# Stick-breaking attention: the sums over later keys from two rounded parts, and scores two heads ahead

## The chip, the cores and the metric

The kernel runs on one core of one Trainium2 chip. The metric is the device time of the whole program in microseconds (us), the median of several runs. A core has TensorE (PE in the rows; its weight loads are PEld), VectorE (DVE), ScalarE (ACT), GpSimd (POOL) and SyncE (SP). They run side by side, each through its own list of instructions in order, and wait for each other on semaphores.

## What is computed

The program is two transformer blocks of two layers each on 512 tokens of width 1024. The change touches one part alone, the stick-breaking attention in the first layer of the second block: 8 heads of dimension 64, 512 queries, 512 keys, in blocks of 128.

```
def stick_breaking_attention(q, k, v):
...
        z = jnp.einsum('bqhd,bkhd->bhqk', q[:, t0:t1], k[:, :t1]) * (HEAD_DIM ** -0.5)
        causal = jnp.arange(t1)[None, :] < (t0 + jnp.arange(SB_BLOCK))[:, None]
        log_fail = jnp.where(causal, -jax.nn.softplus(z), 0.0)
        log_after = lax.cumsum(log_fail, axis=3, reverse=True) - log_fail
        a = jnp.where(causal, jnp.exp(jax.nn.log_sigmoid(z) + log_after), 0.0)
        outs.append(jnp.einsum('bhqk,bkhd->bqhd', a, v[:, :t1]))
```

For each head: scores z, softplus(z), a sum of softplus over all later keys (and the key itself), a = exp(z - that sum), and a times the values. The same layer has eight heads of sliding-window attention beside it, whose output is transposed for the output projection while the stick-breaking heads run.

## The kernel before

Every engine has a program of its own (`pe_sb`, `act_sb`, `dve_sb`), written out by hand in rounds i. Nothing reorders it: what stands first in an engine's list runs first, and an instruction that waits holds up all that is behind it. `K.at(key)` names the semaphore count at which a result is there. PE writes to 8 PSUM banks, handed out in a ring; a bank is reused once DVE or ACT has freed it.

A head has, with keys on the partitions and queries along the row, 1280 columns: 512 + 384 + 256 + 128 for the key blocks 0 to 3, which fill three banks (`SB_BANKS`). Its steps:

- `sb_scores(h)`, PE: per bank one matmul that adds the causal mask and the matmuls of keys by queries, into `sb_z`.
- `dve_zs(h)`, DVE: three copies of the scores from PSUM into z. z has four buffers, s two (`sb_mem`).
- ACT: Abs, Exp, a table load, Ln, on all 1280 columns: s = log(1 + exp(-|z|)), key `sb_ln`.
- DVE: s = max(z, 0) + s, which is softplus, key `sb_sp`.
- `sb_after(h)`, PE: the sum over later keys, ten fp32 matmuls over 2560 columns in all, with a triangle of ones within a key block and a matrix of ones for the blocks after it. An fp32 matmul has two records in the trace.
- DVE: z = z - that sum, three pieces, key `sb_loga`. ACT: a table load and Exp, key `sb_a`.
- `sb_product(h)`, PE: four fp32 matmuls of values by a, 64 rows of bank `abT` 4 + h // 2; two heads fill one.

Beside it `pe_ab_turn(k)`, k 0 to 3, transposes a quarter of the sliding-window output on PE into bank `abT` k, and each of the eight `abT` is taken out by ACT (`act_ab_hi`, a copy rounded to fp32r, the rounded form that TensorE takes in one pass) and then by DVE (`dve_ab_lo`, the rest of it). `sb_blocks(i)` says which k ACT and DVE take out at the head of round i.

In round i of before, PE does after(i-1), product(i-2), turn(i-1) and scores(i+1). ACT does `act_ab_hi` of the blocks, then Abs to Ln of head i, then Exp of head i-1. Block k < 4 is taken out in round k+2. Heads, blocks and rounds count from 0; "after(i)" below is `sb_after` of head i, "hi(k)" is `act_ab_hi` of block k, "ln(i)" is ACT's row Abs, Exp, table load, Ln of head i.

Of the kernel before, what the change touches and what calls it, by code (L numbers as in the profile page):

```python
# [8 lines left out]
F32 = mybir.dt.float32  # L9
# [6 lines left out]
MUL, ADD, SUB, MAX, MIN = ALU.mult, ALU.add, ALU.subtract, ALU.max, ALU.min  # L16
# [2580 lines left out]
def ab_out(K):  # L2597
    return K.mem(W1, 2048).rearrange("p (t n) -> p t n", n=512)
# [42 lines left out]
def act_ab_proj(a, K):  # L2641
    qk, q5, k5, va, qb5, kb5, vb = ab_mem(K)
    cs, gr, snk, posi, posf, ang, kk, sn, co = ab_small(K)

    def feat(tag, dst, f, by):
        a.wait_ge(*K.at(tag, f, 0))
        a.cp(dst[:, f, :], K.ps(tag, f, 0)[:, :], scale=by).then_inc(*a.sig((tag, "out")))
        a.free(tag, f, 0)

    a.wait_ge(*K.at("ab"))  # L2650
    us = cs[:, 256:384]
    for dst, src in zip(sw_mask(K), (K.ident, cs[:, 0:256])):
        a.cp(dst, src).then_inc(*a.sig("sw_mask"))
    for o, by in ((0, 1.0), (128, 0.0), (256, 0.0), (384, 1.0), (512, 0.0), (640, 0.0), (768, 0.0)):
        a.cp(K.rx[:, 8576 + o:8704 + o], us, scale=by).then_inc(*a.sig("sb_mask"))
    for i, dst in enumerate((sn, co)):
        a.wait_ge(*K.at("ab_ang", i))
        a.act(dst, dst, ACT.Sin).then_inc(*a.sig("ab_sin"))
    a.tile()
    act_tok_out(a, K, "ab_q", range(4), lambda t: qk[:, t, 0:512])  # L2660
    a.tile()
    a.tile()
    for t in range(4):
        ps = K.ps("ab_k", t)
        a.wait_ge(*K.at("ab_k", t))
        a.cp(qk[:, t, 512:640], ps[:, 0:128]).then_inc(*a.sig(("ab_qk", t)))
        a.cp(va[:, t, :], ps[:, 128:256]).then_inc(*a.sig())
        a.free("ab_k", t)
    for f in range(4):
        if f % 2 == 0:  # L2670
            a.tile()
        a.root(K.tmpc[:, 60:70], ("ab", f))
        feat("ab_qb", qb5, f, 0.125)
    for f in range(4):
        if f % 2 == 0:
            a.tile()
        feat("ab_kb", kb5, f, 1.0)
    for k in range(0, 6, 2):
        a.wait_ge(*K.at("ab_T", k))
        a.cp(q5[:, k, :] if k < 4 else k5[:, k - 4, :], K.ps("ab_T", k)[:, :]).then_inc(*a.sig("ab_T_a"))  # L2680
        a.free("ab_T", k)
    for kh in range(2):
        a.tile()
        for t in range(4):
            if kh:
                a.wait_ge(*K.at("ab_vb", t))
                a.cp(vb[:, t, :], K.ps("ab_vb", t)[:, :]).then_inc(*a.sig("ab_vb_out"))
                a.free("ab_vb", t)
            for i in (kh * 8 + t * 2, kh * 8 + t * 2 + 1):
                act_sw(a, K, i)  # L2690
    for i in (16, 17):
        act_sw(a, K, i)
# [90 lines left out]
def sw_mask(K):  # L2783

    return K.rx[:, 8192:8320], K.rx[:, 8320:8576]
# [104 lines left out]

SB_COL = {0: 0, 1: 512, 3: 896, 2: 1024}
SB_BANKS = [(1, 3), (2,), (0,)]
SB_ROUNDS = range(11)


def sb_size(kb):
    return 512 - 128 * kb


def sb_part(j):  # L2900

    o = SB_COL[SB_BANKS[j][0]]
    return slice(o, o + sum(sb_size(kb) for kb in SB_BANKS[j]))


def sb_mask(K, j):

    o, n = ((8576, 512), (8960, 256), (8960, 512))[j]
    return K.rx[:, o:o + n]


def sb_mem(K, h):

    return K.mem(SWW + (6960, 416, 4256, 5536)[h % 4], 1280), K.mem(SWW + (1696, 2976)[h % 2], 1280)


def sb_bank(K, tag, h, j):
    c = sb_part(j)
    return K.ps(tag, h, j)[:, 0:c.stop - c.start]


def sb_scores(p, K, h):
    qk, q5, k5, va, qb5, kb5, vb = ab_mem(K)
    pr = slice(h % 2 * 64, h % 2 * 64 + 64)
    if h == 0:
        p.wait_ge(*K.at("ab_kb", "out"))
        p.wait_ge(*K.at("sb_mask"))
    for j, kbs in enumerate(SB_BANKS):
        b, c = p.bank("sb_z", h, j), sb_part(j)
        p.mm(b[:, 0:c.stop - c.start], sw_mask(K)[0], sb_mask(K, j), True, False)  # L2930
        for kb in kbs:
            o, n = SB_COL[kb] - SB_COL[kbs[0]], sb_size(kb)
            ins = p.mm(b[:, o:o + n], kb5[pr, h // 2, kb * 128:kb * 128 + 128], qb5[pr, h // 2, kb * 128:512], False,
                       kb == kbs[-1])
        ins.then_inc(*p.sig(("sb_z", h, j)))
        p.close("sb_z", h, j)


def sb_after(p, K, h):
    s = sb_mem(K, h)[1]  # L2940
    p.wait_ge(*K.at("sb_sp", h))
    for j, kbs in enumerate(SB_BANKS):
        b = p.bank("sb_after", h, j)
        for kb in kbs:
            o, n = SB_COL[kb] - SB_COL[kbs[0]], sb_size(kb)
            ins = p.mm(b[:, o:o + n], K.tri[1], s[:, SB_COL[kb]:SB_COL[kb] + n], True, kb == 3)
            for k2 in range(kb + 1, 4):
                ins = p.mm(b[:, o + (k2 - kb) * 128:o + n], K.ones, s[:, SB_COL[k2]:SB_COL[k2] + sb_size(k2)], False, k2 == 3)
        ins.then_inc(*p.sig(("sb_after", h, j)))
        p.close("sb_after", h, j)  # L2950


def sb_product(p, K, h):

    vb, a = ab_mem(K)[6], sb_mem(K, h)[0]
    k, pr = 4 + h // 2, slice(h % 2 * 64, h % 2 * 64 + 64)
    if h == 0:
        p.wait_ge(*K.at("ab_vb_out"))
    if h % 2 == 0:
        if h:  # L2960
            p.close("abT", k - 1)
        p.bank("abT", k)
    b = K.ps("abT", k)
    p.wait_ge(*K.at("sb_a", h))
    for kb in range(4):
        n = sb_size(kb)
        ins = p.mm(b[pr, kb * 128:512], vb[:, kb, h * 64:h * 64 + 64], a[:, SB_COL[kb]:SB_COL[kb] + n], kb == 0, kb == 3)
    ins.then_inc(*p.sig(("abT", k) if h % 2 else ("sb_o", h)))
    if h == 7:
        p.close("abT", k)  # L2970


def pe_sb(p, K):
    sb_scores(p, K, 1)
    for i in SB_ROUNDS:
        if 0 <= i - 1 < 8:
            sb_after(p, K, i - 1)
        if 0 <= i - 2 < 8:
            sb_product(p, K, i - 2)
        if 1 <= i < 5:  # L2980
            pe_ab_turn(p, K, i - 1)
        if 2 <= i + 1 < 8:
            sb_scores(p, K, i + 1)


def sb_blocks(i):

    return [k for k in range(8) if i == (k + 2 if k < 4 else 2 * k - 4)]


def act_sb(a, K):
    for i in SB_ROUNDS:
        for k in sb_blocks(i):
            act_ab_hi(a, K, k)
        if i < 8:
            z, s = sb_mem(K, i)
            if i >= 2:
                a.wait_ge(*K.at("sb_after", i - 2, 2))
            a.wait_ge(*K.at("sb_zs", i))
            a.act(s, z, ACT.Abs).then_inc(*a.sig())  # L3000
            a.act(s, s, ACT.Exp, scale=-1.0).then_inc(*a.sig())
            a.act(s, s, ACT.Ln, bias=1.0).then_inc(*a.sig(("sb_ln", i)))
        if 0 <= i - 1 < 8:
            z = sb_mem(K, i - 1)[0]
            a.wait_ge(*K.at("sb_loga", i - 1))
            a.act(z, z, ACT.Exp).then_inc(*a.sig(("sb_a", i - 1)))


def dve_zs(v, K, h):
    z = sb_mem(K, h)[0]  # L3010
    if h >= 4:
        v.wait_ge(*K.at(*(("abT", 4 + (h - 4) // 2) if h % 2 else ("sb_o", h - 4))))
    for j in range(3):
        v.wait_ge(*K.at("sb_z", h, j))
        v.cp(z[:, sb_part(j)], sb_bank(K, "sb_z", h, j)).then_inc(*v.sig(("sb_zs", h)))
        v.free("sb_z", h, j)


def dve_sb(v, K):
    dve_zs(v, K, 0)  # L3020
    for i in SB_ROUNDS:
        for k in sb_blocks(i):
            dve_ab_lo(v, K, k)
        if 0 <= i - 1 < 8:
            z = sb_mem(K, i - 1)[0]
            for j in range(3):
                c = sb_part(j)
                v.wait_ge(*K.at("sb_after", i - 1, j))
                v.tt(z[:, c], z[:, c], sb_bank(K, "sb_after", i - 1, j), SUB).then_inc(*v.sig(("sb_loga", i - 1)))
                v.free("sb_after", i - 1, j)  # L3030
        if i < 8:
            z, s = sb_mem(K, i)
            v.wait_ge(*K.at("sb_ln", i))
            v.stt(s, z, 0.0, s, MAX, ADD).then_inc(*v.sig(("sb_sp", i)))
        if i + 1 < 8:
            dve_zs(v, K, i + 1)

# [1 line left out]
def pe_ab_turn(p, K, k):  # L3041
    p.wait_ge(*K.at("sw_out", 15))
    b = p.bank("abT", k)
    for t in range(4):
        ins = p.tr(b[:, t * 128:(t + 1) * 128], ab_out(K)[:, t, k * 128:(k + 1) * 128])
    ins.then_inc(*p.sig(("abT", k)))
    p.close("abT", k)
# [1396 lines left out]
```

## Time and profile before

| | us |
|---|---|
| median of 3 runs | 4309.4 |
| lowest, highest | 4307.35, 4322.24 |
| the profiled execution | 4309.93 |
| its span, from the first to the last instruction | 4307.7 |
| its stick-breaking part, from scores(1) on PE to the first matmul of the output projection | 2658.5 to 2750.0 |

Times in the rows are microseconds from the span's start unless marked ns. What lies between the span and the time of the execution is 2.2 us. A group of instructions shows the form (partitions x columns) of its first one, so a row of 20 matmuls named 128x384 mixes widths. PEclk is the clock granted to TensorE: 1.00 is 2.4 GHz, 0.50 is 1.2 GHz.

### The profile page before, as it was taken

To read this page: it belongs to the slowest core of one execution; us is meant where nothing else is said; L and a number is where in the kernel's file an instruction comes from. 1 tells how busy PE (TensorE), PEld (TensorE's weight loads), DVE (VectorE), ACT (ScalarE), POOL (GpSimd) and SP (SyncE) were. 2 spreads that over 40 slices of the span, in tenths; PEclk is the share of its full clock that TensorE was granted. 3 is DMA by queue.
4 is the path that set the end of the run, shared out by engine and by line. 5 is a ranking of instruction groups with operands and counts; after the bars stand their busy time and mean duration, and the time that the engine had idled before them with its cause. 6 is when DMAs were issued, how large, how long until landed. Compare 5 with 4: busy or idle time off the path is not lost.

```text
span 4307.7 us, 67439 instructions
## 1 busy us (share of the span) xinstructions
PE 3920.8 (91%) x28266; PEld 3229.7 (75%) x28266; DVE 2097.2 (49%) x3022; ACT 1606.8 (37%) x2639; POOL 561.3 (13%) x628
## 2 busy tenths in 40 slices
PE   6988897878999998988899889989999998899999
PEld 4866785766888776756688676678888887678887
DVE  3545454656212353277423664554655428545564
ACT  3333333333111233164323345644334336544333
POOL 0035303642000001002100000000220003000220
PEclk8978898888999999999899999999999999999999
DMA  4234433131212121102232230131223230322332
GB/s 154 81 129 143 147 96 116 32 109 45 73 59 67 51 85 59 58 2 93 70 94 93 79 87 10 52 118 50 94 93 103 88 115 6 119 69 70 98 98 88
DMA packets 248534, 355.08 MB, mean 82 GB/s; under 512 B 9299, under 2 KB 158502, under 8 KB 247846
## 3 DMA queue, kind: packets, MB, share of 16 engines
q1 hardware_dynamic: 233840, 300.49, 21.7%
q0 software_dynamic: 13840, 50.11, 3.7%
q8 instruction: 222, 3.64, 0.4%
q14 instruction: 82, 0.67, 0.1%
q10 hardware_dynamic: 550, 0.17, 0.0%
HBM read 336.50 MB, written 14.24 MB: 81 GB/s over the span
## 4 chain that ended last, share of the span: by engine, by line
PE 76%; DVE 12%; ACT 7%; POOL 2%; issue 2%; DMA 1%; ACTq 0%; DVEq 0%; SPq 0%; POOLq 0%
PE psum L233 20%; PE psum L234 20%; PE psum L235 20%; PE psum L230 13%; ACT arena L341 3%; DVE arena L264 3%; PE psum L239 3%; DVE rw L264 2%; DVE arena L274 2%; POOL arena L379 1%; ACT arena L345 1%; DVE rx L335 1%; ACT rw L345 1%; DVE arena L278 1%; DVE arena L270 1%
## 5 line engine op out<-in xcount | busy, mean ns | idle before, releaser
L233 PE MATMUL psum<-rx,rw 128*128 128x512 f32 (+2 forms) x2864 | 1047.8, 366 | 61.2 <-DVE rx L335 30.1
L234 PE MATMUL psum<-rx,rw 128*128 128x512 f32 (+2 forms) x2864 | 1029.7, 360 | 0.0
L235 PE MATMUL psum<-rx,rw 128*128 128x512 f32 (+2 forms) x2864 | 1028.2, 359 | 0.0
L230 PE MATMUL psum<-arena 32*32 32x32 f32 (+10 forms) x12982 | 810.3, 258 | 158.0 <-ACT arena L345 63.9
L264 DVE TENSOR_TENSOR rw<-arena,rw 128x2048 fp32r<-128x2048 f32 (+2 forms) x239 | 537.6, 2249 | 846.5 <-ACT rw L345 841.2
L230 PEld LDWEIGHTS psum<-arena 32*32 32x32 f32 (+5 forms) x12982 | 614.8, 142 | 334.1 <-issue 113.9
L345 ACT ACTIVATE rw<-arena 128x2048 fp32r<-128x2048 f32 (+2 forms) x239 | 448.1, 1875 | 769.2 <-PE psum L235 744.4
L233 PE MATMUL psum<-rw,rx 128*128 128x512 f32 (+1 forms) x1720 | 683.0, 397 | 53.0 <-DVE rx L335 35.8
L234 PE MATMUL psum<-rw,rx 128*128 128x512 f32 (+1 forms) x1720 | 676.3, 393 | 0.0
L235 PE MATMUL psum<-rw,rx 128*128 128x512 f32 (+1 forms) x1720 | 675.7, 393 | 0.0
L233 PEld LDWEIGHTS psum<-rx,rw 128*128 128x128 f32 (+1 forms) x2864 | 550.3, 192 | 159.7 <-DVE rx L335 42.6
L234 PEld LDWEIGHTS psum<-rx,rw 128*128 128x128 f32 (+1 forms) x2864 | 551.4, 193 | 80.8 <-issue 4.1
L235 PEld LDWEIGHTS psum<-rx,rw 128*128 128x128 f32 (+1 forms) x2864 | 550.2, 192 | 79.1
L345 ACT ACTIVATE arena<-psum 128x512 f32<-128x512 f32 (+6 forms) x675 | 313.9, 465 | 773.1 <-PE psum L235 415.1
L379 POOL TENSOR_TENSOR arena<-arena 128x512 f32<-128x512 f32 (+5 forms) x300 | 419.6, 1399 | 980.4 <-DVE arena L274 396.5
L233 PEld LDWEIGHTS psum<-rw,rx 128*128 128x128 f32 x1720 | 329.6, 192 | 128.6 <-DVE rx L335 40.8
L341 ACT ACTIVATE arena<-arena 128x512 f32<-128x512 f32 (+11 forms) x476 | 249.5, 524 | 468.6 <-DVE arena L274 219.2
L235 PEld LDWEIGHTS psum<-rw,rx 128*128 128x128 f32 x1720 | 328.9, 191 | 68.6
L234 PEld LDWEIGHTS psum<-rw,rx 128*128 128x128 f32 x1720 | 329.6, 192 | 66.2
L274 DVE SCALAR_TENSOR_TENSOR arena<-arena 128x512 f32<-128x512 f32 (+8 forms) x481 | 353.9, 736 | 44.4 <-ACT arena L341 27.8
L264 DVE TENSOR_TENSOR arena<-arena,psum 128x512 f32<-128x512 f32 (+3 forms) x308 | 151.8, 493 | 312.7 <-PE psum L235 205.1
L239 PE MATMUL psum<-arena 128*128 128x128 f32 (+2 forms) x1284 | 200.6, 296 | 102.7 <-DVE arena L264 32.9
(71 smaller groups left out, 2092.0 us busy)
## 6 DMA issues: line engine op xcount, KB each, us to landing
arena<-in_ffn_w_up SPq DMA_DIRECT2D x66, 1024.0 KB, 5.2
arena<-in_ada_w SPq DMA_DIRECT2D x48, 1024.0 KB, 5.2
arena<-in_ffn_w_down SPq DMA_DIRECT2D x40, 1024.0 KB, 5.0
arena<-in_ffn_w_gate SPq DMA_DIRECT2D x22, 1024.0 KB, 5.3
arena<-in_dn_w_in SPq DMA_DIRECT2D x32, 512.0 KB, 5.3
arena<-in_xa_w_kv SPq DMA_DIRECT2D x16, 1024.0 KB, 5.0
arena<-in_hgrn_w_in SPq DMA_DIRECT2D x16, 1024.0 KB, 5.4
arena<-in_da_w_in SPq DMA_DIRECT2D x12, 1024.0 KB, 5.1
```

Of the source, the lines that this page charges most:

```text
L230: return self.e.matmul(out, l, r, start=start, stop=stop)
L233: self.e.matmul(out, l[0], r[0], start=start, stop=False)
L234: self.e.matmul(out, l[0], r[1], start=False, stop=False)
L235: return self.e.matmul(out, l[1], r[0], start=False, stop=stop)
L239: return self.e.transpose(out, a, self.K.ident[0:k, 0:k])
L264: return self.e.tensor_tensor(out, a, b, op)
L270: return self.e.tensor_scalar(out, a, s1, s2, op0, op1)
L274: return self.e.scalar_tensor_tensor(out=out, in0=a, scalar=s, in1=b, op0=op0, op1=op1)
L278: return self.e.tensor_reduce(out, a, AX.X, op)
L341: return self.e.activation(out, a, f, **kw)
L345: return self.e.activation(out, a, ACT.Copy, **kw)
L379: return self.e.tensor_tensor(out, a, b, op)
```

## The change

Three things are done at once.

- `sb_after` no longer multiplies softplus in fp32. DVE rounds s to fp32r (hi, a cast), subtracts it from s and rounds the rest (lo), and PE does every matmul of the sum twice, with hi and with lo, as fp32r by fp32r copies of the triangle and of the ones, which ACT makes once, long before. Ten fp32 matmuls become twenty fp32r ones. There is one pair hi, lo, so the cast of head i waits until after(i-1) has read it.
- Scores run two heads ahead: PE does scores(i+2) at the head of round i and DVE `dve_zs(i+2)`. after(i) moves from round i+1 to round i, product(i-1) and turn(i) follow it, and ten rounds are left of eleven.
- `sb_blocks` moves up with it: block k < 4 is taken out in round k+1 (before k+2), block k > 3 in round 2k-5 (before 2k-4), still at the head of the round on ACT, ahead of ln(i).

```diff
+    for dst, src in zip(sb_split(K)[1:], (K.tri[1], K.ones)):
+        a.cp(dst, src).then_inc(*a.sig("sb_mask"))
...
+def sb_split(K):
+
+    at = [(9728, 1280), (11008, 1280), (9472, 128), (9600, 128)]
+    hi, lo, here, whole = [K.rx[:, o:o + n] for o, n in at]
+    return (hi, lo), here, whole
...
 def sb_after(p, K, h):
-    p.wait_ge(*K.at("sb_sp", h))
+    p.wait_ge(*K.at("sb_lo", h))
...
-            ins = p.mm(b[:, o:o + n], K.tri[1], s[:, SB_COL[kb]:SB_COL[kb] + n], True, kb == 3)
+            for i, s in enumerate(parts):
+                ins = p.mm(b[:, o:o + n], here, s[:, SB_COL[kb]:SB_COL[kb] + n], i == 0, i == 1 and kb == 3)
...
 def pe_sb(p, K):
     sb_scores(p, K, 1)
     for i in SB_ROUNDS:
+        if i + 2 < 8:
+            sb_scores(p, K, i + 2)
+        if i < 8:
+            sb_after(p, K, i)
         if 0 <= i - 1 < 8:
-            sb_after(p, K, i - 1)
-        if 0 <= i - 2 < 8:
-            sb_product(p, K, i - 2)
-        if 1 <= i < 5:
-            pe_ab_turn(p, K, i - 1)
-        if 2 <= i + 1 < 8:
-            sb_scores(p, K, i + 1)
+            sb_product(p, K, i - 1)
+        if 0 <= i < 4:
+            pe_ab_turn(p, K, i)
...
-    return [k for k in range(8) if i == (k + 2 if k < 4 else 2 * k - 4)]
+    return [k for k in range(8) if i == (k + 1 if k < 4 else 2 * k - 5)]
...
             if i >= 2:
-                a.wait_ge(*K.at("sb_after", i - 2, 2))
+                a.wait_ge(*K.at("sb_lo", i - 2))
...
 def dve_sb(v, K):
+    hi, lo = sb_split(K)[0]
     dve_zs(v, K, 0)
+    dve_zs(v, K, 1)
     for i in SB_ROUNDS:
         for k in sb_blocks(i):
             dve_ab_lo(v, K, k)
...
-            v.stt(s, z, 0.0, s, MAX, ADD).then_inc(*v.sig(("sb_sp", i)))
-        if i + 1 < 8:
-            dve_zs(v, K, i + 1)
+            v.stt(s, z, 0.0, s, MAX, ADD).then_inc(*v.sig())
+            if i:
+                v.wait_ge(*K.at("sb_after", i - 1, 2))
+            v.cp(hi, s).then_inc(*v.sig())
+            v.tt(lo, s, hi.bitcast(F32), SUB).then_inc(*v.sig(("sb_lo", i)))
+        if i + 2 < 8:
+            dve_zs(v, K, i + 2)
+        if i < 8:
+            for j in range(3):
+                c = sb_part(j)
+                v.wait_ge(*K.at("sb_after", i, j))
+                v.tt(z[:, c], z[:, c], sb_bank(K, "sb_after", i, j), SUB).then_inc(*v.sig(("sb_loga", i)))
```

ACT's list at the start of the part, with the semaphores that each waits for. Before: Abs, Exp, table, Ln of head 0, then Abs, table, Exp, table, Ln of head 1, the table and Exp that give a of head 0, and then the first block, hi(0):

```order
L341 ACTIVATE arena<-arena 128x1280 [waits s_act]
L341 ACTIVATE arena<-arena 128x1280 [waits s_act,s_dve]
L341 ACT_TABLE_LOAD
L341 ACTIVATE arena<-arena 128x1280 [waits s_act]
L341 ACT_TABLE_LOAD
L341 ACTIVATE arena<-arena 128x1280 [waits s_act]
L341 ACT_TABLE_LOAD [waits s_act]
L341 ACTIVATE arena<-arena 128x1280 [waits s_dve]
L345 ACTIVATE rx<-psum 128x512 [waits s_act,s_pe]
L341 ACTIVATE arena<-arena 128x1280 [waits s_act,s_dve]
```

Now the same place, from Ln of head 0 on:

```order
L341 ACTIVATE arena<-arena 128x1280 [waits s_act]
L345 ACTIVATE rx<-psum 128x512 [waits s_act,s_pe]
L341 ACTIVATE arena<-arena 128x1280 [waits s_act,s_dve]
L341 ACT_TABLE_LOAD
L341 ACTIVATE arena<-arena 128x1280 [waits s_act]
L341 ACT_TABLE_LOAD
L341 ACTIVATE arena<-arena 128x1280 [waits s_act]
L341 ACT_TABLE_LOAD [waits s_act]
L341 ACTIVATE arena<-arena 128x1280 [waits s_dve]
L345 ACTIVATE rx<-psum 128x512 [waits s_act,s_pe]
L341 ACTIVATE arena<-arena 128x1280 [waits s_act] x2
```

hi(0), the L345 row that waits for PE, moved from behind the Exp of head 0 to ahead of the Abs of head 1, and hi(1) from behind the Exp of head 1 to ahead of the Abs of head 2.

PE's list in the round of after(1). Before, after the fp32 sums, came the product of head 0 (64x512 to 64x128), the transposes of block 1 (L239) and the scores of head 3:

```order
L230 MATMUL psum<-arena 128x384 [waits s_dve]
L230 MATMUL psum<-arena 128x256
L230 MATMUL psum<-arena 128x128 x2
L230 MATMUL psum<-arena 128x256
L230 MATMUL psum<-arena 128x128
L230 MATMUL psum<-arena 128x512
L230 MATMUL psum<-arena 128x384
L230 MATMUL psum<-arena 128x256
L230 MATMUL psum<-arena 128x128
L230 MATMUL psum<-arena 64x512 [waits s_act]
```

Now the sums read rx, in pairs, and the product and the transposes follow them as before:

```order
L230 MATMUL psum<-rx 128x384 [waits s_dve]
L230 MATMUL psum<-rx 128x384
L230 MATMUL psum<-rx 128x256 x2
L230 MATMUL psum<-rx 128x128 x4
L230 MATMUL psum<-rx 128x256 x2
L230 MATMUL psum<-rx 128x128 x2
L230 MATMUL psum<-rx 128x512 x2
L230 MATMUL psum<-rx 128x384 x2
L230 MATMUL psum<-rx 128x256 x2
L230 MATMUL psum<-rx 128x128 x2
L230 MATMUL psum<-arena 64x512 [waits s_act]
```

On PE the order of the steps within a round stays; the numbers of the heads against ACT's and DVE's rounds shift by one.

## Rows read from the trace of the kernel before

**Rows 1.** The page: the span, and TensorE's busy time with its share
```profile
span 4307.7 us, 67439 instructions
...
PE 3920.8 (91%) x28266; PEld 3229.7 (75%) x28266; DVE 2097.2 (49%) x3022; ACT 1606.8 (37%) x2639; POOL 561.3 (13%) x628
```

**Rows 2.** Stretches: length, busy us (count) per engine, PEclk, DMA share, GB/s
```profile
2662.40:2667.70 5.30, 0.07 (x2) 0.03 (x1) 1.49 (x1) 3.66 (x3) 0.00 (x0) 0.77 0.00 0
2667.70:2672.10 4.40, 4.40 (x13) 3.44 (x14) 2.49 (x4) 2.32 (x2) 0.00 (x0) 0.50 0.00 0
2672.10:2750.00 77.90, 77.18 (x296) 44.66 (x295) 39.83 (x55) 57.96 (x50) 0.00 (x0) 1.00 0.00 1
2750.00:2800.00 50.00, 50.00 (x230) 41.64 (x230) 26.22 (x40) 24.92 (x45) 1.81 (x3) 1.00 0.35 111
```

**Rows 3.** The chain that ended last, in this part: start, us, what
```profile
2708.23 25.22 PE psum L230 x89
```

**Rows 4.** Timeline, PE: start, us, what, xcount, [idle before <-releaser]; first block, rounds' scores
```profile
2667.67 6.74 PE L230 MATMUL psum<-arena 128*128 128x384 f32 x20 [5.23 <-DVE arena L274]
...
2674.60 0.47 PE L230 MATMUL psum<-rx 128*128 128x512 f32 x1
...
2685.72 0.48 PE L230 MATMUL psum<-rx 128*128 128x512 f32 x1
```

**Rows 5.** Timeline, PE, short stretches: sums, product, transposes; the part's end
```profile
2678.48 4.60 PE L230 MATMUL psum<-arena 128*128 128x384 f32 x20
...
2683.01 2.37 PE L230 MATMUL psum<-arena 128*64 128x512 f32 x8
...
2685.31 0.66 PE L239 MATMUL psum<-arena 128*128 128x128 f32 x4
...
2740.99 9.05 PE L230 MATMUL psum<-arena 128*128 128x384 f32 x36 [0.72 <-DVE arena L274]
2749.97 0.50 PE L233 MATMUL psum<-rw,rx 128*128 128x512 f32 x1
```

**Rows 6.** Timeline, ACT: Abs and Exp of a head, a table load, and hi
```profile
2679.87 2.57 ACT L341 ACTIVATE arena<-arena 128x1280 f32<-128x1280 f32 x2 [0.35 <-DVE arena L290]
2682.46 1.28 ACT L341 ACT_TABLE_LOAD   x1
...
2687.76 0.60 ACT L345 ACTIVATE rx<-psum 128x512 fp32r<-128x512 f32 x1
2690.44 2.57 ACT L341 ACTIVATE arena<-arena 128x1280 f32<-128x1280 f32 x2 [2.09 <-DVE arena L290]
```

**Rows 7.** Timeline, DVE: softplus of heads 0 and 2
```profile
2666.12 1.49 DVE L274 SCALAR_TENSOR_TENSOR arena<-arena 128x1280 f32<-128x1280 f32 x1 [5.22 <-ACT arena L341]
...
2685.06 1.49 DVE L274 SCALAR_TENSOR_TENSOR arena<-arena 128x1280 f32<-128x1280 f32 x1 [1.25 <-ACT arena L341]
```

**Rows 8.** Timeline, PE: fp32r matmuls of 512, 256 and 128 columns, each with the next
```profile
2590.06 0.39 PE L233 MATMUL psum<-rw,rx 128*128 128x512 f32 x1
2590.29 0.40 PE L234 MATMUL psum<-rw,rx 128*128 128x512 f32 x1
...
2507.73 0.28 PE L233 MATMUL psum<-rw,rx 128*128 128x256 f32 x1
2507.85 0.28 PE L234 MATMUL psum<-rw,rx 128*128 128x256 f32 x1
...
2577.21 0.33 PE L230 MATMUL psum<-rx 128*128 128x128 f32 x1
...
2577.47 0.49 PE L230 MATMUL psum<-arena 64*128 64x128 f32 x2
```

**Rows 9.** Groups by form, DVE, 2600 to 4300: xcount | busy us, mean ns | idle
```profile
L264 DVE TENSOR_TENSOR rw<-arena,rw 128x2048 fp32r<-128x2048 f32 x120 | 275.1, 2293 | 273.6 <-ACT rw L345 270.3
...
L290 DVE COPY arena<-psum 128x512 f32<-128x512 f32 x60 | 41.5, 691 | 80.1 <-PE psum L235 59.9 <-PE psum L230 15.0 <-PE psum L239 2.8
...
L269 DVE TENSOR_SCALAR arena<-arena 128x1024 f32<-128x1024 f32 x24 | 18.1, 754 | 0.8
...
L264 DVE TENSOR_TENSOR rw<-arena,rw 128x1024 fp32r<-128x1024 f32 x4 | 4.9, 1225 | 25.2 <-ACT rw L345 25.2
...
L290 DVE COPY arena<-psum 128x256 f32<-128x256 f32 x8 | 3.4, 425 | 1.5 <-PE psum L230 1.3
```

**Rows 10.** Timeline, ACT: the nine mask copies at the start of the layer
```profile
2496.09 3.16 ACT L345 ACTIVATE rx<-arena 128x128 fp32r<-128x128 f32 x9
```

More of the change, by code:

```diff
@@ L2892 @@
 SB_BANKS = [(1, 3), (2,), (0,)]
-SB_ROUNDS = range(11)
+SB_ROUNDS = range(10)
 def sb_size(kb):
@@ L2939, in sb_after @@
 def sb_after(p, K, h):
-    s = sb_mem(K, h)[1]
-    p.wait_ge(*K.at("sb_sp", h))
+    parts, here, whole = sb_split(K)
+    p.wait_ge(*K.at("sb_lo", h))
     for j, kbs in enumerate(SB_BANKS):
@@ L2945, in sb_after @@
             o, n = SB_COL[kb] - SB_COL[kbs[0]], sb_size(kb)
-            ins = p.mm(b[:, o:o + n], K.tri[1], s[:, SB_COL[kb]:SB_COL[kb] + n], True, kb == 3)
+            for i, s in enumerate(parts):
+                ins = p.mm(b[:, o:o + n], here, s[:, SB_COL[kb]:SB_COL[kb] + n], i == 0, i == 1 and kb == 3)
             for k2 in range(kb + 1, 4):
-                ins = p.mm(b[:, o + (k2 - kb) * 128:o + n], K.ones, s[:, SB_COL[k2]:SB_COL[k2] + sb_size(k2)], False, k2 == 3)
+                for i, s in enumerate(parts):
+                    ins = p.mm(b[:, o + (k2 - kb) * 128:o + n], whole, s[:, SB_COL[k2]:SB_COL[k2] + sb_size(k2)], False,
+                               i == 1 and k2 == 3)
         ins.then_inc(*p.sig(("sb_after", h, j)))
@@ L3023, in dve_sb @@
             dve_ab_lo(v, K, k)
[L3024 to L3030, printed above, removed]
         if i < 8:
@@ L3033, in dve_sb @@
             v.wait_ge(*K.at("sb_ln", i))
-            v.stt(s, z, 0.0, s, MAX, ADD).then_inc(*v.sig(("sb_sp", i)))
-        if i + 1 < 8:
-            dve_zs(v, K, i + 1)
+            v.stt(s, z, 0.0, s, MAX, ADD).then_inc(*v.sig())
[10 more added lines that the diff above has]
+                v.tt(z[:, c], z[:, c], sb_bank(K, "sb_after", i, j), SUB).then_inc(*v.sig(("sb_loga", i)))
+                v.free("sb_after", i, j)
 def pe_ab_turn(p, K, k):
```

## The prediction

> **What bounds the kernel now.** The page says that PE is busy 91% of the span [rows 1], but the change lies in one part, so the part decides. Read the stretches first [rows 2]. From 2672.1 to 2750.0 PE is busy 77.2 of 77.9 us at full clock, while ACT is busy 58.0 and DVE 39.8; in the 50 us behind it PE is busy throughout. The chain of work that ended last agrees: it lies on PE for 25.2 us in one piece [rows 3]. The timeline of PE gives the beat: scores start at 2674.60 and again at 2685.72, one head per 11.1 us [rows 4]. The one large hole is at the start: PE idles 5.23 us for the softplus of head 0, and then the clock is 0.50 for 4.4 us [rows 2, 4]. Where is slack? ACT waits 2.1 us before the Abs of a head [rows 6], DVE 1.25 us before softplus [rows 7]. So shorter PE work pays until another engine, or a loop of waits through several engines, takes 11.1 us or more. That loop has to be looked for, since the change moves steps between rounds.
>
> **The sums on PE.** The old block starts at 2678.48 and the product behind it at 2683.01: 4.53 us [rows 5]. The new one has 20 fp32r matmuls: 2 of 512 columns, 4 of 384, 6 of 256, 8 of 128. From start to start a 512 takes 0.23, a 256 takes 0.12 [rows 8], so 384 lies at 0.175. Of 128 columns only one stands alone: 0.26 to an fp32 matmul behind it [rows 8], which bounds it from above; the four transposes of 128 columns with a weight load each start 0.11 apart ((0.66 - 0.33) / 3, where 0.33 is the length of one [rows 5, 8]). I take 0.11, between 0.07 (the columns alone, half of a 256) and 0.26. Sum: 0.46 + 0.70 + 0.72 + 0.88 = 2.8 us, and 0.2 to the fp32 product: 3.0 us, 1.5 less than before. By PE alone a round would be 11.1 - 1.5 = 9.6 us.
>
> **The new work on DVE.** Softplus takes 1.49 [rows 7]. The subtraction that gives lo has two inputs of 1280 columns; that kind takes 1.225 for 1024 and 2.293 for 2048 [rows 9], so 1.49. The cast of 1280 columns has one input: TENSOR_SCALAR of 1024 takes 0.754 [rows 9], in proportion 0.94 and less for the fixed part, so 0.88; the ceiling is the two-input pace, 1.49. I take 0.88, since it is the single-input row that is like it.
> The Trainium skill says the same ("VectorE: DVE Perf Modes", the perf-mode tier table: an fp32 copy within SBUF runs at two elements per cycle, one with two tensors at one); no run here shows it for an fp32r output. At one per cycle each loop below would be 0.6 us longer.
> Each step adds some 0.04 to 0.1 of waiting. DVE's round: lo of a block 0.79, softplus 1.53, cast 0.92, subtraction 1.55, three copies of scores 0.79 + 0.52 + 0.79, and three subtractions of the same size, 2.1 [rows 7, 9]: 9.0 us. That fits under 9.6.
>
> **The moved steps, and the wait they add.** ACT's hi(k), k < 4, now stands at the head of round k+1, ahead of ln(k+1). It waits for turn(k), which on PE stands behind after(k) and product(k-1). What is queued behind the waiting hi(k) on ACT is ln(k+1), then the Exp of head k; DVE waits for ln(k+1) with softplus, cast and lo of head k+1, and PE for those with after(k+1), with product(k) and turn(k+1) behind it. That closes a loop within one round. Before, hi(k) stood ahead of ln(k+2), and after(k+2) came two rounds later, so that the same steps had 22 us. Once round, at full clock:
>
> - after(k) and the gap: 3.0
> - product(k-1), start to turn(k): 2685.31 - 2683.01 = 2.3 [rows 5]
> - turn(k) 0.66 [rows 5], to ACT 0.1: 0.75
> - hi(k) 0.60 and 0.1 [rows 6]: 0.7
> - Abs to Ln: from 2679.87 to softplus at 2685.06 [rows 6, 7]: 5.2
> - softplus 1.53, cast 0.92, lo 1.55: 4.0
>
> Sum 15.95, say 15.9 us, against 11.1 before and 9.6 for PE alone. PE then idles 6.3 us in each such round, behind scores(k+3).
>
> Which rounds? 0 to 1: no product yet, 15.9 - 2.3 = 13.6. 1 to 2: 15.9. 2 to 3: two blocks (2 and 4) are taken out, 16.5. 3 to 4: 15.9. 4 to 5: hi(5) waits for product(3), which ends round 4 on PE, without a turn: 15.3. 5 to 6: no block; DVE's own row sets it (0.1 to 0.2 to each bank, the last subtraction 0.69, softplus to lo 4.0, after a block of 2.8): some 8.3. 6 to 7: hi(6) waits for product(5): 15.3. Sum 100.8. Tail from after(7): 2.9, the last bank's subtraction 0.8, Exp 1.3, product 2.2: 7.2, where before it was 2749.97 - 2740.99 = 9.0 [rows 5].
>
> Start: softplus of head 0 is ready to run at 2666.12 as before [rows 7]; the second dve_zs and scores(2) (3.9 us) lie in the idle 5.2 us. With cast and lo after(0) starts at 2670.1, 2.4 later than before (2667.67 [rows 4]). So at full clock the part ends at 2670.1 + 100.8 + 7.2 = 2778.1, against 2749.97: 28.1 us later.
>
> **The clock.** After 5.2 us of idling the first block before ran at 0.50 for 4.4 us [rows 2] and took 2674.24 - 2667.67 = 6.6 us to the transposes (6.74 with the overlap [rows 4], where a warm one has 4.60 [rows 5]): 2.1 us lost. Now PE idles 6.3 us or more ahead of after(i) for i = 1 to 5 and 7, and 4 us ahead of after(0), and all that follows, after, product and turn, is in the loop. Seven times 0 to 2.1; I take 1.9, near the one row there is: 13.3. The full-clock sum left the 2.1 of the first block out, so it counts here.
>
> **Small things.** Two more mask copies of 0.34 on ACT (3.16 / 9 [rows 10]), 150 us earlier, where ACT waits now and then: 0 to 0.7, taken as 0.3. No DMA, no POOL or SP work is moved; the loads for the next step wait for the last abT and shift with it. The product of this part is followed by the same full PE row as before, so nothing later gives the time back.
>
> **Sum.** 28.1 + 13.3 + 0.3 = 41.7. The profiled execution took 4309.93, 0.5 over the median; so 4351.6 in such an execution, 4351 for the median.
>
> **Rivals.**
> 1. The loop does not bind, PE does. For it: PE is the busiest engine of the part [rows 2], and every step is there and shorter. It would hold if hi(k) were ready when ACT comes to it; the loop decides from the point at which its sum is over 9.6 us, and it would have to lose 6.3. Against: the order of ACT's list, in which hi(0) stands ahead of the Abs of head 1. Time: start +2.4, seven rounds of 9.3 on average (9.6 with a turn, 9.0 on DVE without) 65, tail 7.2, first block's clock 2.1: the part ends at 2744.5, so 5 us earlier, 4304. This is the case on the other side: not slower.
> [...]
> 2. The loop binds, but PE's clock stays full, since PE works 9.6 of 15.9 us. Against: the one idle of this length went to 0.50 [rows 2]. 4338.
> 3. The loop binds and the narrow fp32r matmuls are no faster than the fp32 ones (0.26 each for 128 columns, 0.32 for 256): 1.5 us more in eight blocks, 4363.
>
> **How the numbers follow.** Forecast 0.75, rival 1 0.10, rival 2 0.08, rival 3 0.05, something else 0.02. Range: the cast at the two-input pace adds 8 x 0.6 = 5, narrow matmuls at 0.07 take 8 x 0.3 = 2.5 off, the clock 13 off or 2 on. From 4335, just under rival 2, to 4363, rival 3. Rival 1 is left out. A measurement of this kernel tells 0.5% (21.5 us) from no change; all loop cases are beyond it, rival 1 is within: slower 0.89, same 0.09, faster 0.02.
>
> **What would show it.** In the profile after: PE idle of some 6 us ahead of each after(i), released by DVE; ACT idle ahead of the L345 copies into rx, released by PE (L239, or L230 for the product); a beat of 16 to 18 us in the first five rounds; PEclk under 0.85 over the part; the sums 2.8 us where the clock is full; the cast 0.9. Wrong if the beat is under 11, if ACT does not wait ahead of hi(k), or if the sums take over 4 us at full clock.

## The result, and the profile after

| | before | after |
|---|---|---|
| median, us (5 runs each) | 4307.35 | 4349.04 |
| lowest, highest | 4294.20, 4322.24 | 4342.35, 4352.89 |
| the profiled execution | 4309.93 | 4349.75 |
| its part: scores(1) to the output projection | 2658.5 to 2750.0, 91.5 long | 2656.2 to 2793.05, 136.8 long |

The changed kernel takes 1.0094 times as long (a ratio of the runs' means; 95% interval 1.0072 to 1.0115), 41.7 us more by the medians and 39.8 more between the profiled executions. The part itself grew by 45.3 us. It began 2.3 us earlier, and what lies behind it took some 3 us less; both lie outside the change, and no cause was looked for. That work wanders by several microseconds from run to run: over all the profiled runs here scores(1) starts between 2647.9 and 2658.5. So below each version is judged by two things, its time and the length of its part in the trace; the second is the sharper.

The page after, against [rows 1]: PE is busy 6.6 us more, at 90% where it was 91%. At this height nothing is to be seen.

```profile
span 4347.5 us, 67450 instructions
...
PE 3927.4 (90%) x28266; PEld 3245.1 (75%) x28266; DVE 2114.4 (49%) x3038; ACT 1608.2 (37%) x2641; POOL 562.4 (13%) x628
```

The stretches tell it, with the columns of [rows 2]: length, busy us (count) of PE, PEld, DVE, ACT, POOL, then the granted clock. First scores to after(0), then after(0) to the end of the part, then the 50 us behind it.

```profile
2656.20:2667.80 11.60, 7.88 (x24) 3.62 (x24) 7.72 (x10) 5.10 (x4) 0.00 (x0) 0.92 0.00 0
2667.80:2793.00 125.20, 80.82 (x295) 56.90 (x295) 56.75 (x70) 60.27 (x51) 0.00 (x0) 0.74 0.00 1
2793.00:2843.00 50.00, 50.00 (x230) 41.59 (x229) 26.10 (x40) 24.80 (x45) 1.81 (x3) 1.00 0.35 110
```

Before, from the end of its half-clocked first block on, PE was busy 77.2 of 77.9 us at clock 1.00. Now it is busy 80.8 of 125.2 at 0.74, and no other engine is busy for half of that stretch. No engine is full, so each must be waiting for another. The table of waits (engine, line, waited for: us in total, times, longest) names the circle:

```profile
PE psum L230 <- DVE rx L264: 48.1, 8, 9.8
ACT rx L345 <- PE psum L239: 38.3, 4, 10.2
DVE arena L274 <- ACT arena L341: 28.1, 6, 5.8
...
ACT rx L345 <- PE psum L230: 18.5, 2, 9.6
```

PE waits for DVE's L264 (lo), DVE's softplus (L274) for ACT's L341 (Ln), and ACT's hi (L345) for PE's transposes (L239) four times and for a product (L230) twice. One turn of it, from the timelines of PE, ACT and DVE (start, us, what, [idle before <- who ended it]), answering to [rows 4 to 7]:

```profile
2684.62 5.34 PE L230 MATMUL psum<-rx 128*128 128x384 f32 x20 [7.41 <-DVE rx L264]
2689.89 2.37 PE L230 MATMUL psum<-arena 128*64 128x512 f32 x8
2692.19 0.66 PE L239 MATMUL psum<-arena 128*128 128x128 f32 x4
...
2702.63 4.91 PE L230 MATMUL psum<-rx 128*128 128x384 f32 x20 [6.08 <-DVE rx L264]
```

```profile
2692.88 0.60 ACT L345 ACTIVATE rx<-psum 128x512 fp32r<-128x512 f32 x1 [9.31 <-PE psum L239]
2693.51 2.58 ACT L341 ACTIVATE arena<-arena 128x1280 f32<-128x1280 f32 x2
```

```profile
2698.70 1.49 DVE L274 SCALAR_TENSOR_TENSOR arena<-arena 128x1280 f32<-128x1280 f32 x1 [4.50 <-ACT arena L341]
2700.22 0.83 DVE L290 CAST rx<-arena 128x1280 fp32r<-128x1280 f32 x1
2701.08 1.49 DVE L264 TENSOR_TENSOR rx<-arena,rx 128x1280 fp32r<-128x1280 f32 x1
```

Read it as a relay. after(1) starts at 2684.62, product(0) at 2689.89, turn(1) at 2692.19; hi(1) can start at 2692.88, after ACT has stood for 9.31 us; Abs of head 2 follows at 2693.51, softplus at 2698.70, and lo releases after(2) at 2702.63. The four legs are 8.26 + 0.63 + 5.19 + 3.93 = 18.0 us, the whole beat, with no slack in between. The heads' sums start at 2667.8, 2684.6, 2702.6, 2720.8, 2739.5, 2756.8, 2766.7 and 2783.3: beats of 16.8, 18.0, 18.2, 18.6, 17.3, 9.9 and 16.6, where before had 11.1 [rows 4].

### The profile page after: what moved, and what is told of

Read it like the earlier page. It is cut to its first block, busy times and chain, and to the rows that moved or that the text cites. A ratio compares the mean times of both kernels' runs of the same rounds, so it can differ in the third digit from the quotient of the medians.

```text
span 4347.5 us, 67450 instructions
## 1 busy us (share of the span) xinstructions
PE 3927.4 (90%) x28266; PEld 3245.1 (75%) x28266; DVE 2114.4 (49%) x3038; ACT 1608.2 (37%) x2641; POOL 562.4 (13%) x628
## 4 chain that ended last, share of the span: by engine, by line
PE 76%; DVE 12%; ACT 7%; POOL 2%; issue 2%; DMA 1%; ACTq 0%; DVEq 0%; SPq 0%; POOLq 0%
PE psum L233 20%; PE psum L234 20%; PE psum L235 20%; PE psum L230 13%; ACT arena L341 3%; DVE arena L264 3%; PE psum L239 3%; DVE arena L274 2%; DVE rw L264 2%; DVE rx L335 1%; POOL arena L379 1%; ACT arena L345 1%; ACT rw L345 1%; DVE arena L278 1%; ACT rx L345 1%
## 5 line engine op out<-in xcount | busy, mean ns | idle before, releaser
L264 DVE TENSOR_TENSOR rw<-arena,rw 128x2048 fp32r<-128x2048 f32 (+2 forms) x239 | 537.6, 2249 | 846.4 <-ACT rw L345 841.1
L230 PE MATMUL psum<-arena 32*32 32x32 f32 (+10 forms) x12822 | 781.1, 257 | 150.4 <-ACT arena L345 60.4
L230 PEld LDWEIGHTS psum<-arena 32*32 32x32 f32 (+4 forms) x12822 | 594.7, 142 | 312.2 <-issue 106.6
L345 ACT ACTIVATE rw<-arena 128x2048 fp32r<-128x2048 f32 (+2 forms) x239 | 448.1, 1875 | 766.9 <-PE psum L235 739.7
L345 ACT ACTIVATE arena<-psum 128x512 f32<-128x512 f32 (+6 forms) x675 | 314.3, 466 | 767.2 <-PE psum L235 404.4
L341 ACT ACTIVATE arena<-arena 128x512 f32<-128x512 f32 (+11 forms) x476 | 249.5, 524 | 461.7 <-DVE arena L274 223.3
L274 DVE SCALAR_TENSOR_TENSOR arena<-arena 128x512 f32<-128x512 f32 (+8 forms) x481 | 354.5, 737 | 64.5 <-ACT arena L341 47.8
L264 DVE TENSOR_TENSOR arena<-arena,psum 128x512 f32<-128x512 f32 (+3 forms) x308 | 151.8, 493 | 323.6 <-PE psum L235 206.1
L239 PE MATMUL psum<-arena 128*128 128x128 f32 (+2 forms) x1284 | 201.3, 296 | 97.9 <-DVE arena L264 30.8
```

Of the source, the lines that this page charges most:

```text
L230: return self.e.matmul(out, l, r, start=start, stop=stop)
L239: return self.e.transpose(out, a, self.K.ident[0:k, 0:k])
L264: return self.e.tensor_tensor(out, a, b, op)
L274: return self.e.scalar_tensor_tensor(out=out, in0=a, scalar=s, in1=b, op0=op0, op1=op1)
L341: return self.e.activation(out, a, f, **kw)
L345: return self.e.activation(out, a, ACT.Copy, **kw)
```

## The experiments

In all of them the profile's part is measured from scores(1) to the first matmul of the output projection. Times are medians, of 4 runs for e2, e3 and e6 and of 10 to 12 for e1, e4, e5 and e8; the kernel before had 4305.2 beside the first four, 4305.4 beside the last three (23 runs each). The row "after" is the comparison above, 5 runs against 5 of before at 4307.35. A beat is the time from the start of one head's sums to the start of the next one's.

| | time, us | ratio (95%) | part, us | beats |
|---|---|---|---|---|
| before | 4305.2, 4305.4 | | 91.5 | 10.8 11.1 11.1 11.1 10.8 10.7 7.6 |
| after | 4349.0 | 1.0094 (1.0072 to 1.0115) | 136.8 | 16.8 18.0 18.2 18.6 17.3 9.9 16.6 |
| e1 after, blocks late | 4298.0 | 0.9983 (0.9973 to 0.9993) | 89.3 | 10.0 9.5 9.5 13.5 9.1 8.5 10.2 |
| e2 before, blocks early | 4345.1 | 1.0092 (1.0071 to 1.0113) | 132.3 | 15.7 17.5 17.9 16.9 16.4 13.1 14.4 |
| e3 after, fp32 sums | 4339.9 | 1.0077 (1.0058 to 1.0095) | 128.7 | 15.4 17.6 18.0 16.8 16.4 9.4 14.3 |
| e4 before, split alone | 4310.9 | 1.0011 (1.0000 to 1.0022) | 100.4 | 12.5 12.3 10.2 11.2 12.1 10.3 11.2 |
| e5 e1, another bank | 4298.4 | 0.9985 (0.9974 to 0.9996) | 85.4 | 10.0 9.5 9.5 11.1 9.2 8.5 8.7 |
| e6 after, PE's idle filled | 4332.7 | 1.0062 (1.0045 to 1.0079) | 121.1 | 14.6 17.3 16.3 15.7 15.1 8.2 15.1 |
| e8 two ahead alone | 4301.5 | 0.9983 (0.9973 to 0.9994) | 89.1 | 10.3 11.1 11.1 12.8 10.7 7.8 7.0 |

The theory is that of the prediction: one line of the change, the round in which ACT takes out the blocks, closes the loop, and PE's clock adds to it. The rival is that the slower part comes of the split (more work on DVE) or of the scores two ahead.

### e1_late_blocks: the whole change, with the blocks back in their rounds

```diff
-    return [k for k in range(8) if i == (k + 1 if k < 4 else 2 * k - 5)]
+    return [k for k in range(8) if i == (k + 2 if k < 4 else 2 * k - 4)]
...
-SB_ROUNDS = range(10)
+SB_ROUNDS = range(11)
```

> The changed kernel with one line undone: the blocks are taken out in the rounds of before (k+2 for k below 4, 2k-4 above), eleven rounds; scores two ahead and the rounded parts stay. Loop theory: hi(k) then has two rounds' time, the loop of 15.9 us is gone, the beat falls from 17 to 18 us to the 9.6 us of PE (9.4 in DVE's rounds), the part ends 0 to 9 us earlier than in the kernel before, time 4298 to 4309, ratio to before 0.998 to 1.000, some 42 us under the changed kernel. Rival (the rounded parts or the scores ahead are what costs, the blocks' round is beside the point): the beat stays at 17 us, time near 4349, ratio 1.009.

Measured: 4298.0 us, ratio 0.9983, the part 89.3 us. One line, with the eleventh round that it needs, takes 47.5 us out of the part, and what is left of the change is slightly faster than before. Of the 7.2 us that the time wins over the kernel before, the part shows 2.2; the rest lies outside it and its cause was not looked for. A round from after(2) on, PE's timeline, then the stretch of that round (PE, PEld, DVE, ACT, POOL busy, clock):

```profile
2684.24 2.98 PE L230 MATMUL psum<-rx 128*128 128x384 f32 x20
2687.15 2.37 PE L230 MATMUL psum<-arena 128*64 128x512 f32 x8
2689.45 0.66 PE L239 MATMUL psum<-arena 128*128 128x128 f32 x4
...
2693.74 2.98 PE L230 MATMUL psum<-rx 128*128 128x384 f32 x20
2699.10 3.27 PE L230 MATMUL psum<-arena 128*64 128x512 f32 x8 [2.37 <-DVE rx L335]
```

```profile
2684.20:2693.70 9.50, 9.50 (x44) 5.97 (x43) 8.45 (x12) 8.23 (x8) 0.00 (x0) 1.00 0.00 0
```

PE is full, the clock 1.00, and the round 9.5 us: what the prediction worked out for PE alone (9.6). DVE with 8.45 and ACT with 8.23 are not far behind. The first row also measures the sums at full clock, 2.91 us from their start to that of the product.

The last row of the timeline shows a hole of 2.4 us, for L335, DVE's lo of a block. product(2) opens a new bank for its pair of heads; the code first closes the pair before (block 4) and so is handed just that bank by the ring, which ACT and DVE must empty first. It makes the fourth beat 13.5 where its neighbours have 9.5 and 9.1. e5 below takes this up.

### e2_early_blocks_alone: the kernel before, with only the blocks moved

```diff
-    return [k for k in range(8) if i == (k + 2 if k < 4 else 2 * k - 4)]
+    return [k for k in range(8) if i == (k + 1 if k < 4 else 2 * k - 5)]
```

> The kernel before with only the blocks taken out one round earlier; fp32 sums, scores one ahead. Loop theory: sums 4.5 + product 2.3 + transposes 0.75 + hi 0.7 + Abs to Ln 5.2 + softplus 1.6 = 15.1 us in the rounds with a turn, 4 us of idle PE in each; the part ends 23 us later at full clock, 39 us later if the clock falls each time: ratio 1.005 to 1.009. Rival (the blocks' round does not matter by itself): the beat stays at 11.1, ratio 1.000.

Measured: 4345.1 us, ratio 1.0092, the part 132.3. The same line alone, with none of the rest, makes nearly all of the loss: 40.8 of 45.3 us of the part, slightly over the 39 expected with a low clock. PE's timeline of the round of after(2) (sums and product are fp32 here and stand in one row; the view ends soon after the start of after(3), so the last row has only its first matmuls) and ACT's row in it:

```profile
2690.32 9.25 PE L230 MATMUL psum<-arena 128*128 128x384 f32 x28 [3.74 <-DVE arena L274]
2699.49 0.66 PE L239 MATMUL psum<-arena 128*128 128x128 f32 x4
...
2708.24 2.07 PE L230 MATMUL psum<-arena 128*128 128x384 f32 x3 [4.38 <-DVE arena L274]
```

```profile
2700.19 1.23 ACT L345 ACTIVATE rx<-psum 128x512 fp32r<-128x512 f32 x2 [8.81 <-PE psum L239]
```

It is the same relay: PE to ACT's L345 by the transposes, ACT to softplus, softplus (here without cast and lo) back to PE. The sums are longer by their fp32 form and the way over DVE is shorter, and so the beat is about that of after.

### e3_fp32_sums: after without the split

```diff
-            v.stt(s, z, 0.0, s, MAX, ADD).then_inc(*v.sig())
-            if i:
-                v.wait_ge(*K.at("sb_after", i - 1, 2))
-            v.cp(hi, s).then_inc(*v.sig())
-            v.tt(lo, s, hi.bitcast(F32), SUB).then_inc(*v.sig(("sb_lo", i)))
+            v.stt(s, z, 0.0, s, MAX, ADD).then_inc(*v.sig(("sb_sp", i)))
...
 def sb_after(p, K, h):
-    p.wait_ge(*K.at("sb_lo", h))
+    p.wait_ge(*K.at("sb_sp", h))
...
```

Behind that stand the ten fp32 matmuls of before again.

> The changed kernel with the sums back in fp32 from softplus itself (no cast, no lo, ten matmuls); scores two ahead and early blocks stay. Loop theory: the loop loses 2.4 us on DVE and gains 1.7 us on PE, 15.1 us; with a start 2.4 us earlier the part ends 21 us (full clock) to 34 us later than before: ratio 1.005 to 1.008, 10 us under the changed kernel. Rival (the rounded parts cost the 42 us): ratio 1.000.

Measured: 4339.9 us, ratio 1.0077, the part 128.7. That is 37.2 us over the kernel before, beyond the 34 expected. Within the loop the split costs 8.1 us of the part (136.8 against 128.7), some 1 us a head: 2.4 us of cast and lo come in, while the sums save 1.6 us at full clock. So the rival, that the split costs the 42 us, fails: 37.2 of the part's 45.3 are there without it. And where the loop decides, cutting PE's work lengthens the part, since the cut is paid for by another engine in the same loop.

### e4_split_alone: the kernel before with the split and its masks

```diff
-            v.stt(s, z, 0.0, s, MAX, ADD).then_inc(*v.sig(("sb_sp", i)))
+            v.stt(s, z, 0.0, s, MAX, ADD).then_inc(*v.sig())
+            hi, lo = sb_split(K)[0]
+            v.cp(hi, s).then_inc(*v.sig())
+            v.tt(lo, s, hi.bitcast(F32), SUB).then_inc(*v.sig(("sb_lo", i)))
...
 def sb_after(p, K, h):
-    p.wait_ge(*K.at("sb_sp", h))
+    p.wait_ge(*K.at("sb_lo", h))
...
```

Behind that stand the twenty fp32r matmuls of after.

> The kernel before with the rounded parts alone; scores one ahead, blocks in the rounds of before. Theory: PE needs only 9.4 us a round, but with scores one ahead another loop appears: the copies of scores on DVE stand behind lo, so copies 2.1 + Abs to Ln 5.2 + softplus, cast and lo 4.0 = 11.3 us per head in every round; the part ends 9 us later than before, ratio 1.002. Rival (PE's shorter sums pay at once): the beat falls to 9.6, 8 us earlier, ratio 0.998.

Measured: 4310.9 us, ratio 1.0011 with an interval from 1.0000 to 1.0022, the part 100.4 against 91.5. PE has 1.6 us less to do per head, and the part is longer. The timelines of ACT and DVE show the other loop, in which PE has no leg at all:

```profile
2677.11 2.58 ACT L341 ACTIVATE arena<-arena 128x1280 f32<-128x1280 f32 x2 [2.74 <-DVE arena L290]
...
2688.33 2.58 ACT L341 ACTIVATE arena<-arena 128x1280 f32<-128x1280 f32 x2 [2.73 <-DVE arena L290]
```

```profile
2682.30 1.49 DVE L274 SCALAR_TENSOR_TENSOR arena<-arena 128x1280 f32<-128x1280 f32 x1 [1.19 <-ACT arena L341]
2683.83 0.83 DVE L290 CAST rx<-arena 128x1280 fp32r<-128x1280 f32 x1
2684.69 1.49 DVE L264 TENSOR_TENSOR rx<-arena,rx 128x1280 fp32r<-128x1280 f32 x1
2686.28 2.01 DVE L290 COPY arena<-psum 128x512 f32<-128x512 f32 x3
```

Abs at 2677.11, softplus at 2682.30 (5.19), cast and lo to 2686.28 (3.98), the copies of the next head's scores to 2688.33 (2.05), and there stands the next Abs: 11.22 us. ACT waits for the copies, the copies stand behind lo, and lo waits through softplus for ACT. As long as the scores are copied only one head ahead, this loop stands above the 9.6 that PE alone could have.

### e5_other_bank: e1, and the new bank is taken before the old one is closed

```diff
-        if h:
-            p.close("abT", k - 1)
         p.bank("abT", k)
+        if h:
+            p.close("abT", k - 1)
```

> The changed kernel with the blocks in the rounds of before (as in the first experiment) and, beside it, the bank of a new pair of heads handed out before the old one is given back. In the first experiment product(2) waited 2.4 us for DVE to take out block 4, whose bank it had been given, and the clock fell behind it: the one round of 13.6 us between beats of 9.5. Theory: that wait goes, the round falls to 9.5 to 11, the part ends 1 to 4 us earlier: time 4294 to 4298, ratio to before 0.9975. Rival (the wait was one for the Exp of head 2, put down to DVE by the trace): the round stays at 13.6, ratio 0.9983.

Measured: 4298.4 us, ratio 0.9985, the part 85.4 us, the shortest of all. In the trace the hole ahead of product(2) shrinks from 2.37 to 1.58 us, and the clock stays full over it, so the product takes 2.37 and not 3.27. What is left of the hole is the wait for block 2, whose bank the ring hands out now and which DVE takes out just ahead of block 4:

```profile
2694.50 2.98 PE L230 MATMUL psum<-rx 128*128 128x384 f32 x20
2699.05 2.37 PE L230 MATMUL psum<-arena 128*64 128x512 f32 x8 [1.58 <-DVE rx L335]
```

The part is 3.9 us shorter than in e1 (2.4 in this beat, which is 11.1 where 9.5 to 11 was expected, and 1.5 in the last), but the times of the two kernels, 4298.4 and 4298.0, don't tell them apart: 3.9 us is 0.09%, less than either interval.

### e6_filled: after, with PE kept busy while it waits for lo

Matmuls of 512 columns (12 ahead of after(0), 22 ahead of each of the next five, then 8 and 38) go into the bank that the sums then overwrite. They add work and change no result.

```diff
     for j, kbs in enumerate(SB_BANKS):
         b = p.bank("sb_after", h, j)
+        if j == 0:
+            for _ in range((12, 22, 22, 22, 22, 22, 8, 38)[h]):
+                p.mm(b[:, 0:512], sw_mask(K)[0], sb_mask(K, 0), True, True)
+            p.wait_ge(*K.at("sb_lo", h))
```

> The changed kernel, blocks early as in it, with fill: PE does 8 to 38 more fp32r matmuls of 512 columns (0.23 us each, 12 before head 0, 22 before heads 1 to 5, 8 before head 6, 38 before head 7) into the bank of the sums ahead of each wait for lo; the sums overwrite them. They lie in PE's idle time and are 1 us shorter than it. Theory (the clock is a term of the loop, 1.9 us a round): the beat falls to 15.9 in the five long rounds, PEclk is 1.00 over the part but for its start, the part ends 13 us earlier than in the changed kernel: time 4336, ratio to before 1.0065. Rival (the low clock lies beside the loop, the excess over 15.9 is waiting): the beat stays at 17 to 18.6, time 4349, ratio 1.009 to 1.010.

Measured: 4332.7 us, ratio 1.0062, the part 121.1, 15.7 us shorter than after with more work in it. The stretch from after(0) to the end of the part (clock 0.98 in place of 0.74), and PE's timeline from after(1) to the start of after(2), where the view ends:

```profile
2664.00:2773.90 109.90, 101.63 (x451) 70.95 (x451) 57.07 (x71) 60.36 (x51) 0.00 (x0) 0.98 0.00 1
```

```profile
2678.95 4.58 PE L230 MATMUL psum<-rx 128*128 128x384 f32 x20 [2.19 <-DVE rx L264]
...
2690.05 5.30 PE L230 MATMUL psum<-rx 128*128 128x512 f32 x22
2696.21 1.03 PE L230 MATMUL psum<-rx 128*128 128x384 f32 x6 [0.85 <-DVE rx L264]
```

PE still waits for lo at the end of each filling, so the filling delays nothing, and the beats are the loop's own at full clock: 14.6, 17.3, 16.3, 15.7, 15.1, 8.2 and 15.1. Only the second still holds a stretch at half clock, 3.4 us inside after(1), whose sums take 4.5 us to the product where e1 has 2.91. So the clock makes at least 15.7 us of the part's 45.3, and some 17.3 with the 1.6 us that e6 still loses there; the rest is the loop without the clock.

### e8_ahead_fp32: scores two ahead alone

e3 with the two edits of e1 and e5: fp32 sums, no cast and lo, the blocks late, the scores two heads ahead.

> Scores two ahead alone: sums in fp32 from softplus, blocks in the rounds of before, the other bank as in the run beside it. Theory: PE bounds with 11.1 us a round as in the kernel before, since the sums are as long; the start loses nothing; so the part ends 0 to 4 us earlier than before, ratio 0.999 to 1.000, 4305 to 4301. Rival (scores ahead bring the gain seen in the first experiment, the rounded sums nothing): ratio 0.998, the beat under 10.

Measured: 4301.5 us, ratio 0.9983, slightly below the expected 0.999 to 1.000, the part 89.1. The stretch from after(2) to after(3), at 2685.3 and 2696.5 (PE, PEld, DVE, ACT, POOL busy, clock), shows a plain round of it:

```profile
2685.30:2696.50 11.20, 11.20 (x45) 6.49 (x44) 5.79 (x8) 8.30 (x8) 0.00 (x0) 1.00 0.00 0
```

PE is full at clock 1.00, and the round is as long as before, 11.1 us, and so is the one ahead of it. The start, from scores(1) to after(0), is 9.2 us in both. The 2.4 us that the part wins are 0.5 in the first beat and 3.6 in the last two, less 1.7 in the fourth, which has a hole of 1.6 us ahead of product(2) as in e5. Of e5's 6.1 us, then, neither half gives the whole: the split alone adds 8.9, the scores two ahead alone take 2.4 off, both together take 6.1 off. In time, e8 and e5 can't be told apart.

## Why the prediction held, and where its sizes were off

The forecast was 4351, the measurement 4349.04; the range held it, and slower by over 0.5% is what came. The mechanism is the one that was forecast. That the number came this near is in part luck: in the part the forecast had 41.4 us more and 45.3 came, while between the profiled executions the work outside the part, to which the forecast gave 0.3 us, took 5.5 us less. By its steps, in the part:

| step | predicted | measured |
|---|---|---|
| scores(1) to after(0) | 11.6 | 11.6 |
| sums, at full clock, to the product (e1) | 3.0 | 2.91 |
| cast; lo | 0.88; 1.49 | 0.83; 1.49 |
| Abs to softplus; softplus to after | 5.2; 4.0 | 5.19; 3.93 |
| turn to hi, hi to Abs | 0.75; 0.7 | 0.69; 0.63 |
| beats at full clock (e6) | 13.6 15.9 16.5 15.9 15.3 8.3 15.3 | 14.6 17.3 (1.6 of it half clock) 16.3 15.7 15.1 8.2 15.1 |
| tail at full clock (e6) | 7.2 | 7.4 |
| the clock | 13.3 | 15.7 (after less e6), 17.3 with e6's own 1.6 |
| the part | 132.9 | 136.8 |

- **What bounds**: PE before, the loop after. Shown: ACT stands 9 to 10 us ahead of every hi but those of block 4, which follows at once on block 2's, and of block 7 at the end, for PE's transposes (for a product where the block has none), PE 6 to 10 us ahead of all but two of the sums, and e1 and e2 take the loop away and put it in with one line.
- **Rival 1** (PE decides, 4304) would have needed hi to be ready when ACT comes to it. e1 makes that so, and takes 4298.0.
- **Rival 2** (the clock stays full, 4338) fell: the granted clock is 0.74 over the part. e6, which forces its condition, gives 4332.7.
- **Rival 3** (narrow fp32r matmuls no faster) fell: in e1 the twenty take 2.9 us. Its bound of 0.26 for 128 columns was far off, and its price was too low for its own figures: 0.26 for 128 columns and 0.32 for 256 make the sums 2.4 us longer, not 1.5, which would have been some 4370.
- **The clock's term was the mis-sized one.** It took 2.1 us from the one half-clocked block before, an fp32 one, and let one of eight blocks pass as free. In the trace after, all eight blocks run wholly or in good part at 0.50, after(1) for one (columns of [rows 2]), and sums and product take 7.6 us together behind after(1) (2684.62 to 2692.19), where e1's warm round has 5.2 (2684.24 to 2689.45).

```profile
2679.60:2689.80 10.20, 5.18 (x20) 4.99 (x20) 6.73 (x8) 3.60 (x3) 0.00 (x0) 0.50 0.00 1
```

From the start of the sums to what follows them the eight take 5.1, 5.3, 4.8, 5.3, 5.2, 5.1, 3.9 and 5.3 us, and a warm one 2.8 to 2.9. With two products that were slowed too (2.9 for 2.4), the seven blocks that the forecast priced lost 2.3 us each and not 1.9, and after(6) with its product 1.6, which was put at nothing. Together that is 17.8; the way over e6 gives 17.3, against 13.3, and this is all of the 3.9 us by which the part was longer than forecast. The same term was too small in e2 (39 expected, 40.8 measured), e3 (34, 37.2) and e6 (13, 15.7). The range's upper side had only 2 us for it.
- **The rest came out even, by two errors.** The first beat was 14.6 for 13.6, and e6's ACT timeline shows why: Abs and Exp of head 1 are apart, with a table load of 1.28 us between them, where later heads have both in one piece ([rows 6], Abs and Exp as one x2). The list of ACT ahead of the prediction shows this load; the sum took Abs to Ln as 5.2 for every head and left it out. Against it the other beats, without the half clock in the second, are 0.1 to 0.2 under their sums. At full clock the part would be 119.5 us (e6's 121.1 less 1.6); the forecast had 119.6.

```profile
2668.55 1.27 ACT L341 ACTIVATE arena<-arena 128x1280 f32<-128x1280 f32 x1
2669.84 1.28 ACT L341 ACT_TABLE_LOAD   x1
2671.13 1.27 ACT L341 ACTIVATE arena<-arena 128x1280 f32<-128x1280 f32 x1
```

- **Not told by the traces**: the 0.3 us for the two mask copies. Nothing so small shows in a time that wanders by 5 us.

The Trainium skill bore on this twice. "Perfetto Trace Analysis", Identifying the Most-Contended Engine, says to optimize the engine with the highest occupancy first. By matmul busy time that was PE, 99% of the stretch in [rows 2], and the split shortens PE's work; once the loop is gone the beat does fall (9.5 in e1), while after and e4 are longer with less PE work in them. The same section does not take matmul busy time as TensorE's measure, though, but the share of weight loads beside the FLOPs: here 57% (44.66 of 77.9), less than ACT's 74% (57.96 of 77.9). So the rule named no clear engine here, and it prices no wait that goes round through several. "VectorE: DVE Perf Modes", the perf-mode tier table, has the fp32 copy within SBUF at two elements per cycle; the cast with an fp32r output took 0.83 us for 1280 columns, against 1.49 for two tensors, so the trace agrees.

## What to carry to other kernels

Before moving a step to an earlier round, write down what is queued behind it on its engine and follow that around until it comes back to the step: if the circle closes within one round and its sum is more than any engine's own work in a round, that sum is the new beat, whatever the engines' busy shares say. A step that only empties a buffer belongs where its input has long been done, and not ahead of the work that makes the next input. Cutting the busiest engine pays little when a loop through the others stands right behind it: here the split made the part longer by itself (e4) and shorter only together with the scores two ahead and the blocks left late (6.1 us in e5, of which the scores alone give 2.4 in e8). In time, e1, e5 and e8 are all 0.15 to 0.17% faster than before and can't be told apart, so what the split adds shows in the part alone.

## What the runs showed beyond that

A wait in front of TensorE is paid for twice. The idle that the loop causes lets the clock fall to 0.50, and since the sums and the product behind it lie in the loop, their slowness lengthens the round as well. It goes no further: PE's idle ahead of the sums did not grow from round to round (7.4, 6.1, 6.7, 6.1 and 5.9 us ahead of after(1) to after(5)). Filling the idle with useless matmuls won 15.7 us of the part, and 16 us of the time (4332.7 against 4349.0). It is no remedy, since taking the loop away wins 51, but it measures the clock's share by itself.
